# Value products of softmax attentions in two halves, and the exponential one unit further ahead

## What is computed

```python
def mla_block(qn, qr, kn, kr, v):                       # layers 0 and 1 of the first block, 6 heads, all keys
    s = (einsum('bqhd,bkhd->bhqk', qn, kn) + einsum('bqhr,bkr->bhqk', qr, kr)) * MLA_SCALE
    p = softmax(s, axis=-1)
    return einsum('bhqk,bkhd->bqhd', p, v)

def block(args):                                        # swa_latent: 6 heads, context and a window of 3 tiles
    ...
    s_loc = where(valid, einsum('bqgrd,bkgd->bgrqk', q_b, k_b) * SWA_SCALE, -inf)
    s_ctx = einsum('bqgrd,bcgd->bgrqc', q_b, k_ctx) * SWA_SCALE
    p = sink_softmax(concatenate([s_ctx, s_loc], axis=-1), sink)
    return einsum('bgrqc,bcgd->bqgrd', p[..., :n_ctx], v_ctx) + einsum('bgrqk,bkgd->bqgrd', p[..., n_ctx:], v_b)
```

## Time and profile before

| | us |
|---|---|
| median of 3 runs | 5046.98 (5033.56 to 5055.67) |
| the profiled execution | 5051.52 |
| its span, first to last instruction | 5049.6 |
| TensorE busy | 4289.3 (85%) |
| VectorE busy | 1992.1 (39%) |
| ScalarE busy | 1113.3 (22%) |

### The profile page before, as it was taken

How to read it: one execution, slowest core, us unless ns; L and a number is a source line. 1 busy time by engine, 2 the same in 40 slices (tenths; PEclk the granted TensorE clock), 3 DMA queues, 4 the chain that set the end, 5 groups by cost and what they waited for, 6 DMA issues and landing times. The chain is left out here.

```text
span 5049.6 us, 59760 instructions
## 1 busy us (share of the span) xinstructions
PE 4289.3 (85%) x22943; PEld 2841.9 (56%) x22943; DVE 1992.1 (39%) x3727; ACT 1113.3 (22%) x2167; POOL 794.5 (16%) x811
## 2 busy tenths in 40 slices
PE   6997886978999698988859989997778484999996
PEld 4664555436777565556338867674556433444443
DVE  1224554144444322556144432114866714333332
ACT  1113344131111111335021111112443211011111
POOL 0110000302332111000201210003410101122221
PEclk9998998988999899999979999999999586999998
DMA  6114011267776413200179963104411012999997
GB/s 236 44 46 111 16 45 54 82 261 253 248 253 208 132 58 101 53 25 21 41 286 356 335 228 136 53 29 112 121 52 56 1 38 79 343 334 338 332 336 244
DMA packets 367280, 769.60 MB, mean 152 GB/s; under 512 B 60116, under 2 KB 136572, under 8 KB 365816
## 3 DMA queue, kind: packets, MB, share of 16 engines
q1 hardware_dynamic: 336888, 653.85, 37.3%
q0 software_dynamic: 24432, 90.30, 7.2%
q10 hardware_dynamic: 5712, 22.02, 1.1%
HBM read 650.60 MB, written 115.51 MB: 152 GB/s over the span
## 5 line engine op out<-in xcount | busy, mean ns | idle before, releaser
L3205 PE MATMUL bexp_gu<-bexp_wu,bexp_xT 128*128 128x512 f32 x1024 | 452.8, 595 | 8.0 <-DMA bexp_wu<-in_w_expert_up 4.8
L3205 PEld LDWEIGHTS bexp_gu<-bexp_wu,bexp_xT 128*128 128x128 f32 x1024 | 193.1, 191 | 239.4 <-issue 239.4
L3193 PE MATMUL bexp_acc<-bexp_wd,bexp_hid 128*128 128x512 f32 x512 | 225.1, 592 | 1.0 <-ACT bexp_hid L3147 1.0
L618 PE MATMUL p_ring<-p_hT,p_wc 128*128 128x256 f32 x1008 | 221.3, 382 | 4.9 <-DMA p_wc<-in_w_in 4.9
L618 PEld LDWEIGHTS p_ring<-p_hT,p_wc 128*128 128x128 f32 x1008 | 192.9, 192 | 31.9 <-issue 5.2
L626 PE MATMUL p_ring<-p_wt,p_hT 128*128 128x400 f32 (+2 forms) x480 | 170.8, 516 | 0.0
L2001 PE MATMUL l0exp_gu<-l0exp_xT,l0exp_wg 128*128 128x160 f32 x1024 | 166.2, 319 | 4.5 <-DVE l0exp_xT L2045 4.5
L2001 PEld LDWEIGHTS l0exp_gu<-l0exp_xT,l0exp_wg 128*128 128x128 f32 x1024 | 154.8, 204 | 11.6 <-issue 6.2
L3232 DVE TENSOR_SCALAR bexp_ex<-bexp_ex 128x512 f32<-128x512 f32 x32 | 15.6, 489 | 368.7 <-ACT bexp_ex L3159 368.7
L1108 PE MATMUL l0mla_scores<-l0mla_kT,l0mla_qT 96*128 96x512 f32 (+1 forms) x312 | 142.6, 545 | 21.1 <-DMA l0mla_qT<-RT 15.0
L3193 PEld LDWEIGHTS bexp_acc<-bexp_wd,bexp_hid 128*128 128x128 f32 x512 | 94.9, 190 | 108.9 <-issue 107.6
(11 more groups left out here) (665 smaller groups left out, 8345.9 us busy)
## 6 DMA issues: line engine op xcount, KB each, us to landing
bexp_wu<-in_w_expert_up SPq DMA_DIRECT2D x64, 2048.0 KB, 20.7
bexp_wd<-in_w_expert_down SPq DMA_DIRECT2D x32, 2048.0 KB, 7.9
l0exp_wg<-in_exp_w_gate SPq DMA_DIRECT2D x16, 2048.0 KB, 8.6
l0exp_wu<-in_exp_w_up SPq DMA_DIRECT2D x16, 2048.0 KB, 14.2
l0exp_wd<-in_exp_w_down SPq DMA_DIRECT2D x16, 2048.0 KB, 8.4
l1exp_wg<-in_exp_w_gate SPq DMA_DIRECT2D x16, 2048.0 KB, 9.7
l1exp_wu<-in_exp_w_up SPq DMA_DIRECT2D x16, 2048.0 KB, 14.0
l1exp_wd<-in_exp_w_down SPq DMA_DIRECT2D x16, 2048.0 KB, 9.9
```

The costliest lines, as they stand in the source:

```text
L618: mm = nc.tensor.matmul(out[:, i * PC:(i + 1) * PC], wc[:, k, b * 128:(b + 1) * 128], hT[ch % 2][:, k, :], start=(k == 0), stop=(k == KD - 1))
L3193: mm = nc.tensor.matmul(acc[c][:, :], hid[j][:, f, :], wd[j][:, f, c * 512:(c + 1) * 512], start=(f == 0), stop=(f == KF - 1))
L3205: mm = nc.tensor.matmul(gu[h][:, :], xT[j][:, k, :], wu[j][h][:, k, :], start=(k == 0), stop=(k == KD - 1))
```

## The change

`mix` gets a second argument: half 0 (the first blocks, one more if their number is odd) runs at the even unit of the next pair, where the whole ran before, with all the waits; half 1 runs at the odd unit, behind its first group, without a wait, and signals `mixed_s`. `out` moves from the end of VectorE's even unit to the end of the odd one. The probabilities get `NBUF` buffers, and ScalarE issues the exponential of unit u + NBUF - 1 behind the copy of u: with three buffers u + 2, with two u + 1 as before.

```diff
-        prob = [sb(f"prob{j}", [128, NBLK * 128]) for j in range(2)]
+        prob = [sb(f"prob{j}", [128, NBLK * 128]) for j in range(NBUF)]
...
-                def mix(pt):
+                def mix(pt, half):
                     u = 2 * pt
-                    pe.wait_ge(taken_a, START + takes_a[first_group[u + 2]])
-                    pe.wait_ge(taken_v, START + takes_v[first_group[u + 2]])
-                    pe.wait_ge(outed, START + pt)
...
-                    for j, b in enumerate(bl):
+                    middle = (len(bl) + 1) // 2
+                    if half == 0:
+                        pe.wait_ge(taken_a, START + takes_a[first_group[u + 2]])
+                        pe.wait_ge(taken_v, START + takes_v[first_group[u + 2]])
+                        pe.wait_ge(outed, START + pt)
...
+                    for j in range(middle) if half == 0 else range(middle, len(bl)):
                         for a in range(2):
...
-                    mm.then_inc(mixed_s, 1)
+                    if half == 1:
+                        mm.then_inc(mixed_s, 1)
...
-                        if i == 0 and u % 2 == 0 and u:
-                            mix(u // 2 - 1)
-                mix(PT - 1)
+                        if i == 0 and u >= 2:
+                            mix(u // 2 - 1, u % 2)
+                mix(PT - 1, 0)
+                mix(PT - 1, 1)
...
-                    if u >= 2:
-                        act.wait_ge(turned, START + first_group[u - 1])
+                    if u >= NBUF:
+                        act.wait_ge(turned, START + first_group[u - NBUF + 1])
...
-                exps(0)
+                for u in range(NBUF - 1):
+                    exps(u)
                 for u in range(U):
...
-                    if u + 1 < U:
-                        exps(u + 1)
+                    if u + NBUF - 1 < U:
+                        exps(u + NBUF - 1)
...
-                    if u % 2 == 0 and u:
+                    if u % 2 == 1 and u >= 3:
                         out(u // 2 - 1)
```

More of the change, by code:

```diff
@@ L1120, in turn @@
                         if j < n:
-                            src = prob[u % 2][:, j * 128:(j + 1) * 128]
+                            src = prob[u % NBUF][:, j * 128:(j + 1) * 128]
                         else:
@@ L1126, in turn @@
                     tp.then_inc(turned, 1)
-                def mix(pt):
+                def mix(pt, half):
                     u = 2 * pt
-                    pe.wait_ge(taken_a, START + takes_a[first_group[u + 2]])
-                    pe.wait_ge(taken_v, START + takes_v[first_group[u + 2]])
-                    pe.wait_ge(outed, START + pt)
-                    p = work[u][0]
-                    if work[u][2] == 0 and (p == 0 or not v_once):
-                        pe.wait_ge(v_in[p], START + parts_in.get(v_in[p].num, 0))
-                    bl = blocks(u)
-                    for j, b in enumerate(bl):
+                    bl = blocks(u)
+                    middle = (len(bl) + 1) // 2
[3 more added lines that the diff above has]
+                        pe.wait_ge(outed, START + pt)
+                        p = work[u][0]
+                        if work[u][2] == 0 and (p == 0 or not v_once):
+                            pe.wait_ge(v_in[p], START + parts_in.get(v_in[p].num, 0))
+                    for j in range(middle) if half == 0 else range(middle, len(bl)):
                         for a in range(2):
-                            mm = nc.tensor.matmul(mixed[a * DK:(a + 1) * DK, 0:128], v[0 if v_once else work[u][0] % 2][a][:, b, :],
+                            mm = nc.tensor.matmul(mixed[a * DK:(a + 1) * DK, 0:128], v[0 if v_once else work[u][0] % 2][a][:, bl[j], :],
                                                   probT[pt % 2][:, a * len(bl) + j, :], start=(j == 0), stop=(j == len(bl) - 1))
-                    mm.then_inc(mixed_s, 1)
+                    if half == 1:
+                        mm.then_inc(mixed_s, 1)
                 for u in range(min(NBUF, U)):
@@ L1177, in exps @@
                         nc.scalar.activation(sunk[pt % 2][:, a:a + 1], sinks[:, h:h + 1], ACT.Exp, bias=shift[u % NBUF][:, :]).then_inc(sunk_s, 1)
-                    nc.scalar.activation(prob[u % 2][:, 0:nk], scores[u % NBUF][:, 0:nk], ACT.Exp, bias=shift[u % NBUF][:, :],
+                    nc.scalar.activation(prob[u % NBUF][:, 0:nk], scores[u % NBUF][:, 0:nk], ACT.Exp, bias=shift[u % NBUF][:, :],
                                          scale=scale, accum_out=total[pt % 2][:, a:a + 1]).then_inc(raised, 1)
```

## The result

Timed beside each other, the changed kernel took 4997.0 us (median of four, 4988.0 to 5012.9) and the one before 5043.1 (four, 5033.6 to 5055.7): ratio 0.9922, interval 0.9898 to 0.9946. (The ratio on record is not the quotient of the two medians, 0.9909, which lies in the interval too.) Laid on the forecast's own base of 5046.98 us that is 5007.6 us, a gain of 39 where 26 were forecast; the range of 5003 to 5045 holds it, and the whole interval lies beyond 0.5%. The profiled execution of after took 5012.85 us (span 5010.8), the one of before 5051.52: 38.7 less. The five stages give 39.3 of that. The rest of the program, which no run here edits, took 4054.5 and 4055.0 in these two executions; that it agrees so closely is luck, since it took between 4041 and 4058 in the ten profiled ones.

The account below looks back on a forecast made before the run. In five attention stages (997.4 of 5049.6 us), TensorE's pace and its waits for ScalarE's copy, the exponential and VectorE's copy decide. Window -32, MLA +9, neighbourhood -3 make -26 off 5046.98: 5021 us, range 5003 to 5045.

Parts of the forecast that it names:

- Rival (a): Window pairs bound by VectorE's copy at 0.3 us gain, MLA's seams unfilled: -2, 5045 us; chance 0.21 together with (d).
- the term for the context pairs: First-layer window stage: six context pairs, with what the queue's start gives, gain 6 us (bounds 0 and 9).
- the one that read 15.1 us of waits in 32: First window stage: of 15.1 us score waits for the exponential, 24 at 0.30 are 7.2, eight others hold 7.9.
- the pair's price: MLA stages: splitting the products adds an uncovered 0.35 us per steady latent pair, +16 us over 46 pairs.
- the price that the two sizes gave: Visits of 20 and 40 products imply a fixed price, some 0.33 us per visit, whatever the number of products.
- the four places: MLA, where head pairs meet or a stage ends: the half visit fills waits of about 1 us each, -4 us.
- -3 for the clock: MLA: filling gaps may avoid the granted clock's fall, nothing to -9 us; -3 taken.
- The step that put nothing on the start: Neighbourhood stage's beginning: second exponential waits for a bias ahead of the first copy; TensorE needs that bias too, so 0.
- rival (b): ScalarE's exponential waits for VectorE's shift ahead of the next copy; window units stall 0.5 us each: +28, 5075 us; chance 0.06.
- The edits at no cost: VectorE's moved final multiplication (0.28 us), SyncE's later loads, GpSimd's spreading and the third probability buffer cost nothing.
- (c): Visits cost less and the clock stays: 0.65 us per window pair, MLA +3, sum -40 + 3 - 6, 5004 us; chance 0.13.
- (d): Exponential ahead brings nothing in window stages, leaving some -4 there: total +2, 5049 us; chance 0.21 together with (a).

Follow-up runs that it names:

- e2: Changed kernel with the products left whole at the even unit, so only the exponential runs further ahead; ratio 0.9948 to the kernel before.
- e3: Changed kernel with only the MLA stages' products whole again at the even unit; ratio 0.9925 to the kernel before.
- e1: Changed kernel with the exponential only one unit ahead and two probability buffers, products still in halves; ratio 0.9995 to the kernel before.
- e6: Changed kernel with MLA's halves behind the second group and the exponential further ahead in the window stages only; ratio 0.9822 to the kernel before.

## Why the prediction was right or wrong

**Window pair: right in each step.** 5.31 to 5.33 against 5.33; visits 0.80 and 0.59 against 0.80 and 0.58; 0.11 lost to VectorE's copy against 0.1. Rival (a)'s mechanism, VectorE's copy as the new bound, came in at this 0.11 and no more.

**Window stages: -39.9 instead of -32; the term for the context pairs was mis-sized.** The first layer gave 25.0 us, of which 24 pairs at 0.54 are 13: 12 for context pairs, starts and ends where I took 6. The steps show where. A head pair in the middle of the stage (two context pairs, eight latent ones) went from 54.6 to 46.7 us, 7.9 where eight pairs at 0.54 give 4.3: 3.5 for the context pairs and the first and last tiles beside them, over 10 in three head pairs. About 1.2 more is clock, not the change: at the stage's end before took two steps of 5.64 and 5.74 at a granted 0.95 and 0.75, its repeat 5.45 and 4.73 at 1.00. The step that failed is the one that read 15.1 us of waits in 32. Those are matmul rows, and they hold less than the wait. The weight load of a score waits for the same exponential, and shows more; sums of waits of before (us, times, longest):

```profile
PEld l0swa_scores L1108 <- ACT l0swa_prob L1178: 23.4, 38, 1.4
PEld l1swa_scores L1108 <- ACT l1swa_prob L1178: 12.7, 22, 1.1
```

One of them as matmul and as weight load, in a context pair of before, with the score ahead of it:

```profile
753.25 0.60 PE L1108 MATMUL l0swa_scores<-l0band_k,l0swa_qT 128*128 128x256 f32 x2
754.63 0.70 PE L1108 MATMUL l0swa_scores<-l0band_k,l0swa_qT 128*128 128x256 f32 x2 [0.78 <-ACT l0swa_prob L1178]
...
754.63 0.30 PEld L1108 LDWEIGHTS l0swa_scores<-l0band_k,l0swa_qT 128*128 128x128 f32 x2 [1.19 <-ACT l0swa_prob L1178]
```

From start to start it is 1.38 (753.25 to 754.63) for 256 columns that cost 0.44: 0.94 lost, between the two brackets. The matmul's modelled end hides 0.16 of it, as it did in the steady pair (0.30 in the earlier trace rows, 0.46 from start to start), and the restart of 0.10 comes on top. By the weight loads the first stage waits 10.7 us more than the second, near the 10.1 by which its gain is larger (10.4 in e2); with the clock set aside the excess is some 9. In the second window stage, 14.9 us instead of 13, the rest is the first and last tiles, four pairs where two head pairs meet that went from 22.4 to 19.9, 0.63 each instead of 0.54, and the stage's second step, which the earlier exponential cuts from 5.46 to 3.65.

**MLA: +2.4 instead of +9; the pair's price was right, the places where head pairs meet and stages end were mis-sized.** A pair costs 0.30 more, not 0.35. The visit has the price that the two sizes gave, uncovered, and does not go with the number of products. The Trainium skill (TensorEngine Tiling (Array Packing), section Key Properties) has TensorE drain at a change of mode; this 0.30 agrees with it, but no run parts a drain from what else a visit costs. The steps of both stages, after against before, give the sum to rounding:

| | forecast | measured |
|---|---|---|
| steady pairs | +16 (46 at 0.35) | +12.9 (43 steps at 0.30) |
| the four places, where head pairs meet or a stage ends | -4, and -3 for the clock | -7.9 where head pairs meet, -5.1 at the two ends |
| beginnings of the two stages | 0 | +2.4 |

So the terms that failed are those of the four places: -13 where I had -7. A place where head pairs meet is worth 2.0 with the full clock, and not 1 (three steps took 22.06 in e3 and 20.08 in after), and the clock's fall cost another 4.0 at the two of before, where I took 3 for all four. At the ends cover and clock can't be parted: the last steps took 13.49 and 13.40 at a granted 0.75 in before, 10.91 twice at 1.00 in after. How much of the clock's part the change brings each time stays open: the first stage is shorter by 4.4 here, by 2.8 repeat against repeat, and by 0.8 and 0.6 against e3 and e2, whose clock fell at the end but not where head pairs meet. What makes it fall in one execution and not in another wasn't tried. The second stage's +6.8 meets the forecast (23 pairs at 0.35 less one place of 1 is +7) in part by luck: its first step took 12.10 instead of 9.46, at a granted 0.51, and its last 2.5 less. In the repeats, +6.3, the first differs by 0.1 and the last by 0.3.

**Neighbourhood: -1.8, and -4.3 repeat against repeat, around the -3.** The steady pair is 3.50 + 3.39 = 6.89 (6.95 forecast). The step that put nothing on the start was wrong: the stage's first two steps took 19.4 and 18.5 us in after and its repeat, 17.0 and 17.1 in before and its repeat. With the exponential ahead alone (e2) they took 18.5, with halves alone (e1, e6) 18.5 and 18.1, so both edits cost something there. For the exponential it is rival (b)'s mechanism, in one place: ScalarE stands in its queue before a shift that waits for a bias, with the copy behind it.

**The edits at no cost** stayed so: the steady pairs leave no room for the moved multiplication, and no new wait shows in them. **Sum:** -39.9 + 2.4 - 1.8 = -39.3 against -26. The stated range holds it because it reached toward (c); the narrower -15 to -37 is missed by 2, since the window term came out 7.9 lower and the MLA term 6.6 lower. **Rivals:** (a) fell with the window pair, (d) with e1 and e2: the exponential ahead gives most of it. (b) didn't decide anywhere but at that one start: in both window stages together TensorE's matmuls wait 0.3 us for ScalarE's copy, once. (c) is nearest in total (5004 against 5007.6), and its +3 for MLA came out; but its window pair had VectorE's wait gone, which it isn't, and its -40 for the window stages was reached by the context pairs.

## What to carry to other kernels

When two waits in one pair hang on one engine's queue, their covers don't add up (0.31 and 0.43 us a pair alone, 0.55 together): price both edits together. Put filler work behind the group whose copy TensorE actually waits for, in each unit that waits: a visit that covers nothing cost 0.3 us here, one at the right place gave 0.6. Read a wait from start to start: of 0.94 us the matmul's row showed 0.78, and its weight load 1.19.

## What was not expected of the hardware

The granted TensorE clock at one place of the same kernel, with the same work ahead of it (TensorE busy 9.12 of 10 us twice, then 7.21 or 6.91), was 0.89 and 0.62 in one execution and 1.00 in another, worth 2.35 us over the two steps there (10.09 and 7.46 against 9.33 and 5.87). In that other execution it fell at the next such place. With the products in halves it fell at none of ten. A term for it belongs into the range, not into the sum, as long as one execution alone shows it; and one repeat that differs does not show that the change has no part in it.
